# A new order of the vector and scalar engines' work, and a later inverse transfer, in the softmax attention of a two-block kernel

## The reference

```
first block:  stick-breaking attention (8 heads), and "MLA" attention (8 heads):
    z = q k^T * 96**-0.5 ; p = softmax(where(allowed, z, -inf)) ; o = p v
    y_mla = (o * silu(gate_mla)) @ w_o_mla
second block: "fox" attention (16 heads of 64):
    s = q k^T + c_q - c_k ; masked to k_pos <= q_pos ; p = softmax(s) ; o = p v ; m = o @ w_out
then MLPs, a short convolution, gates and norms
```

## Time and profile before

| | |
|---|---|
| time, median of 3 runs | 1698.45 us (1698.14 to 1699.87) |
| profiled execution | 1698.45 us, its span 1696.5 us |
| busy share of the span | PE 99%, PEld 85%, DVE 76%, ACT 56%, POOL 10% |
| granted TensorE clock | 0.998, 9 tenths or more in all 40 slices of the page |
| exponentials (L2197) | 96, the first at 300.2 us, the last at 659.6 us |
| spread inverses (L2219) | 24 transfers, 311.0 to 664.2 us |

### The profile page before, as it was taken

One profiled execution on the slowest core, in us unless ns is written; L12 is line 12 of the kernel. 1 busy time (PEld: TensorE's weight loads), 2 busy tenths in 40 slices (PEclk: granted clock), 3 DMA queues, 4 the chain that ended last, 5 costly groups with the idle time before them and its releaser, 6 DMA issues.

```text
span 1696.5 us, 25098 instructions
## 1 busy us (share of the span) xinstructions
PE 1673.9 (99%) x9279; PEld 1440.2 (85%) x9279; DVE 1287.2 (76%) x2054; ACT 951.4 (56%) x1717; POOL 169.8 (10%) x147
## 2 busy tenths in 40 slices
PE   9999999999999999999999999999999999999998
PEld 7888877888788887789999997778887989999977
DVE  6378877876568888688888986685556969898966
ACT  4267875665436666476646365642125766564555
POOL 2011212000300000310000002320003000000041
PEclk9999999999999999999999999999999999999999
DMA  8222124324243333344232343323232432332621
GB/s 269 86 75 75 40 69 107 85 66 149 75 113 88 87 89 94 94 176 128 75 105 95 125 174 112 112 75 100 99 99 107 156 100 100 100 108 92 242 69 50
DMA packets 158163, 180.72 MB, mean 107 GB/s; under 512 B 22121, under 2 KB 130182, under 8 KB 156262
## 3 DMA queue, kind: packets, MB, share of 16 engines
q1 hardware_dynamic: 150790, 159.22, 30.0%
q10 hardware_dynamic: 7264, 20.05, 3.4%
HBM read 161.96 MB, written 12.63 MB: 103 GB/s over the span
## 4 chain that ended last, share of the span: by engine, by line
PE 81%; DVE 10%; ACT 3%; DMA 3%; issue 2%; POOL 1%; DVEq 0%; ACTq 0%; POOLq 0%; SPq 0%
PE bank L1171 24%; PE bank L1172 23%; PE bank L1173 23%; DVE split_weights L2701 2%; DMA raw_weights<-in_w_mlp_down 2%; PE bank L1520 2%; PE bank L1544 1%; PE bank L1439 1%; POOL ssum L3663 1%; DVE act_b L2701 1%; PE bank L1557 1%; DMA inverse_rows<-row_sums 1%; PE bank L1428 1%; DVE act_a L2703 1%; PE bank L1556 0%
## 5 line engine op out<-in xcount | busy, mean ns | idle before, releaser
L1171 PE MATMUL bank<-act_a,split_weights 128*128 128x512 f32 (+1 forms) x1360 | 525.5, 386 | 4.6 <-ACT work L2183 1.4
L1173 PE MATMUL bank<-act_a,split_weights 128*128 128x512 f32 (+1 forms) x1360 | 518.5, 381 | 0.0
L1172 PE MATMUL bank<-act_a,split_weights 128*128 128x512 f32 (+1 forms) x1360 | 518.2, 381 | 0.0
L1171 PEld LDWEIGHTS bank<-act_a,split_weights 128*128 128x128 f32 x1360 | 256.0, 188 | 57.2 <-issue 6.0
L1173 PEld LDWEIGHTS bank<-act_a,split_weights 128*128 128x128 f32 x1360 | 255.6, 188 | 50.3
L1172 PEld LDWEIGHTS bank<-act_a,split_weights 128*128 128x128 f32 x1360 | 256.0, 188 | 44.9 <-issue 0.2
L1171 PE MATMUL bank<-act_b,split_weights 128*128 128x256 f32 (+1 forms) x648 | 207.4, 320 | 2.0 <-DVE split_weights L3395 1.5
L1173 PE MATMUL bank<-act_b,split_weights 128*128 128x256 f32 (+1 forms) x648 | 206.4, 318 | 0.0
L1172 PE MATMUL bank<-act_b,split_weights 128*128 128x256 f32 (+1 forms) x648 | 206.3, 318 | 0.0
L2643 DVE TENSOR_TENSOR split_weights<-raw_weights,split_weights 128x2048 fp32r<-128x2048 f32 x55 | 127.8, 2324 | 76.2 <-ACT split_weights L1882 63.4
L1882 ACT ACTIVATE split_weights<-raw_weights 128x2048 fp32r<-128x2048 f32 x51 | 97.3, 1908 | 119.6 <-PE bank L1173 119.6
(11 more groups left out here) (357 smaller groups left out, 3223.5 us busy)
## 6 DMA issues: line engine op xcount, KB each, us to landing
raw_weights<-in_w_mlp_up SPq DMA_DIRECT2D x32, 1024.0 KB, 5.4
raw_weights<-in_w_mlp_down SPq DMA_DIRECT2D x32, 1024.0 KB, 5.2
raw_weights<-in_w_in SPq DMA_DIRECT2D x18, 1024.0 KB, 5.1
raw_weights<-in_w_conv_in SPq DMA_DIRECT2D x12, 1024.0 KB, 5.1
raw_weights<-in_w_attn_in SPq DMA_DIRECT2D x16, 512.0 KB, 5.1
raw_weights<-in_w_ple_gate SPq DMA_DIRECT2D x8, 1024.0 KB, 5.0
raw_weights<-in_w_out SPq DMA_DIRECT2D x4, 1024.0 KB, 5.9
raw_weights<-in_w_attn_in SPq DMA_DIRECT2D x4, 1024.0 KB, 5.2
```

What stands on the lines that cost most here:

```text
L1171: nc.tensor.matmul(dst, w[0], a[0], start=first, stop=False)
L1172: nc.tensor.matmul(dst, w[0], a[1], start=False, stop=False)
L1173: mm = nc.tensor.matmul(dst, w[1], a[0], start=False, stop=last)
```

## The change

Three things change, and PE's strings are not among them.

A new step f on ACT issues the second head's b transfer of the pair before (it does nothing in pair 0). It stands after p1 (after e2 in fox, after e1 in fox's last pair), and b1 goes from the end of all pairs but MLA's last and fox's last, where it stays.

DVE's k moves from before p2 or m5 to behind m6, and other steps change places around it. In MLA c3 now stands ahead of m7, in fox y1 ahead of p4. Fox's last pair gets new strings on both engines, and output tile 2 (o2) moves into it from the pair before.

The two semaphores of the d transfers become one, which counts all of them.

```
-        inverse_out = [sem(f"inverse_out_{hh}") for hh in range(2)]
+        inverse_out = sem("inverse_out")
...
-        DVE_MLA = "m0 m1 m2 m3 p0 p1 k0 p2 m4 p3 n0 m5 c0 c1 c2 y1 m6 p4 m7 c3 p5 s2 n1 p6 g0 p7 y2 x0 x1 s3 g1"
+        DVE_MLA = "m0 m1 m2 m3 p0 p1 p2 m4 p3 n0 m5 c0 c1 c2 y1 m6 p4 k0 c3 m7 p5 s2 p6 n1 g0 p7 y2 x0 x1 s3 g1"
...
-        DVE_FOX = "m0 m1 c0 m2 c1 p0 m3 s2 p1 m4 k0 m5 p2 p3 n0 y0 m6 c2 m7 c3 p4 p5 y1 n1 g0 p6 p7 x0 x1 s3 g1"
+        DVE_FOX = "m0 m1 c0 m2 c1 p0 m3 s2 p1 m4 m5 p2 p3 n0 y0 m6 k0 c2 m7 c3 y1 p4 p5 g0 n1 p6 p7 x0 x1 s3 g1"
...
-                    act.wait_ge(inverse_out[hh], 16 * (h // 2 + 1))
+                    act.wait_ge(inverse_out, 16 * (h + 1))
...
+                        elif what == "f":
+                            if pair:
+                                inverse_to_half(pair - 1, s)
```

More of the change, by code:

```diff
@@ L460, in hybrid_block_kernel @@
         PE_MLA = "z0 g0 z1 g1 z2 t0 z3 t1 z4 g2 t2 z5 t3 z6 g3 v0 t4 z7 g4 t5 t6 g5 t7 g6 g7 v1"
-        ACT_MLA = "e0 e1 y1 p0 e2 p1 w0 e3 p2 p3 s2 w1 d0 e4 e5 p4 y2 e6 p5 e7 b0 p6 r0 p7 d1 s3 r1 b1"
-        DVE_MLA = "m0 m1 m2 m3 p0 p1 k0 p2 m4 p3 n0 m5 c0 c1 c2 y1 m6 p4 m7 c3 p5 s2 n1 p6 g0 p7 y2 x0 x1 s3 g1"
+        ACT_MLA = "e0 e1 y1 p0 e2 p1 f1 w0 e3 p2 p3 s2 w1 d0 e4 e5 p4 y2 e6 b0 p5 e7 p6 r0 p7 s3 d1 r1"
+        DVE_MLA = "m0 m1 m2 m3 p0 p1 p2 m4 p3 n0 m5 c0 c1 c2 y1 m6 p4 k0 c3 m7 p5 s2 p6 n1 g0 p7 y2 x0 x1 s3 g1"
@@ L463, in hybrid_block_kernel @@
         PE_FOX = "z0 g0 z1 g1 z2 t0 t1 z3 g2 z4 t2 g3 z5 t3 g4 z6 t4 t5 z7 v0 g5 t6 t7 g6 g7 v1"
-        ACT_FOX = "w0 y0 e0 e1 w1 p0 e2 s2 p1 e3 p2 p3 e4 e5 y1 d0 e6 s3 p4 p5 e7 r0 d1 p6 b0 p7 r1 b1"
-        DVE_FOX = "m0 m1 c0 m2 c1 p0 m3 s2 p1 m4 k0 m5 p2 p3 n0 y0 m6 c2 m7 c3 p4 p5 y1 n1 g0 p6 p7 x0 x1 s3 g1"
+        ACT_FOX = "w0 y0 e0 e1 w1 p0 e2 f1 s2 p1 e3 p2 p3 e4 e5 d0 y1 e6 s3 p4 p5 b0 e7 r0 p6 p7 d1 r1"
+        DVE_FOX = "m0 m1 c0 m2 c1 p0 m3 s2 p1 m4 m5 p2 p3 n0 y0 m6 k0 c2 m7 c3 y1 p4 p5 g0 n1 p6 p7 x0 x1 s3 g1"
@@ L468, in hybrid_block_kernel @@
         PE_NEAR = "z0 z1 z2 g0 g1 t0 t1 z3 g2 z4 t2 z5 g3 t3 z6 g4 t4 t5 v0 g5 z7 g6 g7 t6 t7 a0 v1"
-        ACT_NEAR = "y0 e0 e1 p0 p1 e2 w0 w1 e3 p2 p3 e4 e5 e6 d0 o0 o1 p4 p5 y1 r0 e7 o2 b0 p6 p7 d1 s2 r1 b1"
-        DVE_NEAR = "m0 m1 m2 k0 m3 p0 y0 c0 c1 p1 p2 m4 m5 p3 n0 m6 c2 c3 o0 o1 p4 y1 m7 p5 g0 x0 x1 n1 p6 p7 s2 o2"
+        ACT_NEAR = "y0 e0 e1 p0 p1 f1 e2 w0 w1 e3 p2 p3 e4 d0 e5 e6 o0 o1 p4 p5 b0 y1 r0 e7 p6 p7 s2 d1 r1"
+        DVE_NEAR = "m0 m1 m2 m3 p0 y0 c0 c1 p1 p2 m4 m5 p3 n0 m6 k0 c2 c3 o0 o1 p4 y1 m7 p5 g0 x0 x1 n1 p6 p7 s2"
@@ L473, in hybrid_block_kernel @@
         PE_LAST = "z0 z1 z2 g1 t0 z3 t1 g2 t2 t3 z4 z5 z6 g3 t4 z7 g4 v0 t5 g5 t6 t7 g6 v1"
[L474 to L478, removed]
+        ACT_LAST = "e0 s1 p0 e1 f1 y0 e2 o2 e3 p1 o3 w0 p2 y1 o4 p3 e4 o5 d0 w1 e5 o6 e6 e7 b0 p4 p5 d1 r0 p6 p7 b1 r1"
@@ L479, in hybrid_block_kernel @@
+        DVE_LAST = "m0 m1 m2 h1 p0 m3 s1 o2 y0 p1 o3 c0 p2 m4 o4 k0 y1 p3 n0 o5 m5 c1 m6 m7 c2 n1 c3 p4 p5 o6 g0 p6 p7 g1"
+        ACT_MLA_LAST = "e0 e1 y1 p0 e2 p1 f1 w0 e3 p2 p3 w1 d0 e4 e5 p4 o0 e6 b0 p5 o1 e7 p6 r0 d1 p7 o2 b1 r1"
+        DVE_MLA_LAST = "m0 m1 m2 m3 p0 p1 p2 m4 p3 n0 m5 c0 c1 c2 y1 m6 p4 k0 c3 m7 p5 o0 n1 p6 g0 o1 p7 x0 x1 o2 g1"
         EARLY_OUT = {"mla": 3, "fox": 7}
@@ L2211, in inverse_to_row @@
                     nc.scalar.dma_start(inverse_rows[hh, :].rearrange("(p j) -> p j", p=P), pair_sums(i, hh))\
-                        .then_inc(inverse_out[hh], 16)
+                        .then_inc(inverse_out, 16)
                 def inverse_to_half(i, hh):
                     h = heads_before(kind, 2 * i + hh)
-                    act.wait_ge(inverse_out[hh], 16 * (h // 2 + 1))
+                    act.wait_ge(inverse_out, 16 * (h + 1))
                     if i:
```

## The result

| | before | changed |
|---|---|---|
| time, median of 5 runs each | 1698.45 us (1698.14 to 1699.87) | 1707.88 us (1706.91 to 1708.19) |
| profiled execution, its span | 1698.45 us, 1696.5 | 1708.22 us, 1706.3 |

The ratio is 1.0052 with a 95% interval of 1.0038 to 1.0067, which is 6.5 to 11.4 us. The changed kernel is slower, as forecast, but by 9.4 us between the medians and not by 5.0, and 1707.88 lies above the forecast range. The time before is the median of 5 runs, not of 3 as the table ahead of the prediction has it.

The account below looks back on a forecast made before the run. PE, busy 99% of the span, was taken to bound the kernel. Terms 3.45 + 2.0 - 0.95 + 0.5 = +5.0 us on 1698.45 gave 1703.4 us (chance 0.50), range 1696.5 to 1707.

Parts of the forecast that it names:

- MLA, +3.45 forecast: MLA pairs 1 to 3: k and c3 ahead of m7 make t7 late by 1.15 us each, 3 x 1.15 = +3.45.
- it adds nothing: MLA, ACT: b0 waits for k and holds p5 until about 351.6, still earlier than m7, so no cost.
- Fox pairs 1 to 5, +2.0 forecast: Fox, DVE: k behind m6 and y1 ahead of p4 make t6 wait for p4; 0.4 us a pair, +2.0.
- the 0.2 at t7: Fox pairs: about 0.2 us that t7 waited for e7, claimed to be over once t6 starts later.
- b1 becomes f1, -0.95: Fox pair 3: f1 stands late enough that the d transfer is back, -0.95 us; all other pairs 0.
- Pair 6, 0 forecast: Pair before fox's last: o2 leaves, k moves behind m6, DVE had idle time; 0, within 0.3 us.
- Pair 7, +0.5 forecast: Fox's last pair: a new wait at g2 against a better ordered end; first share at 668.9 less 0.2, +0.5 us.
- The wait at g2: Fox's last pair: PE stands still some 2.6 us at g2 for o2's low part, ready at 654.2.
- the 13.3 us from g2 to v1: Fox's last pair: PE's time from g2 to v1, 13.3 us or a little less, putting v1 at about 667.5.
- is better ordered: End of fox's last pair: y1 early and weight quarters ahead of p4 remove v1's 1.44 us wait and 0.26 at 668.18.
- the last pair is worse: Rival, chance 0.16: g2 waits 2.6 us in fox's last pair and later steps do not close up; +7.1, 1705.5 us.
- Behind pair 7, 0 forecast: After fox's last pair: no cost given; weight quarters ahead of p4 were to remove a wait of 0.26 us.

Follow-up runs that it names:

- f1_behind: Changed kernel with f1 behind p2 instead of behind p1 on ACT in MLA; 1707.87 us, ratio 1.0058.
- m7_first: Changed kernel with DVE's row maximum m7 ahead of k and c3 again in MLA; 1709.64 us, ratio 1.0058.
- b0_behind: As m7_first, but on ACT in MLA b0 stands behind p5 and e7 instead of ahead of them; 1707.04 us, ratio 1.0047.
- y1_behind: Changed kernel with DVE's y1 behind p5 instead of ahead of p4 in fox's pairs 0 to 5; 1705.17 us, ratio 1.0038.
- e5_first: Changed kernel with e5 ahead of d0 on ACT in fox's pair 6; 1706.98 us, ratio 1.0047.
- c3_late: Changed kernel with DVE's c3 behind p7 instead of ahead of p4 in fox's pair 7; 1706.72 us, ratio 1.0050.

## Why the prediction was wrong in size

**MLA, +3.45 forecast, +4.3 measured.** The mechanism held: m7 starts at 352.70 where the text had 351.7 for the old start of the pair, which is 0.84 later now, and t7 waits 1.17 and 1.18 us where 1.15 was forecast. Two things were missed. f1's issue takes 0.45 us of ACT, ahead of w0 and e3, which costs 0.5 us over the three pairs (f1_behind). And in pair 3 o1 stands in front of e7, which costs 0.2; no run takes it away. The prediction's sentence on b0, that "it adds nothing", was right for this order only: with m7 ahead of k it becomes the bound (m7_first, b0_behind).

**Fox pairs 1 to 5, +2.0 forecast, +2.4 measured.** t6 waits 0.69 where the text had 0.6, and the 0.2 at t7 goes, as it said. y1_behind shows y1's share: without it t6 waits 0.34 less.

**b1 becomes f1, -0.95.** Right: pair 3 is as long as its neighbours, and no pair gained otherwise.

**Pair 6, 0 forecast, +0.7 measured.** The text looked at o2 and k only. It did not look at d0, which the new string puts ahead of e5, where it waits for n0 (e5_first).

**Pair 7, +0.5 forecast, +2.8 measured.** This is the step that failed. The wait at g2 was forecast as 2.6, and t1 and g2 together start 2.84 later. v1's wait is gone, as forecast. The failed term is the 13.3 us from g2 to v1, which rest on the sentence that the end of the pair "is better ordered": they took 15.16. t6 waits 1.1 us, for p4 behind b0 and c3. And behind the wait at g2 the clock fell, 1.4 us, for which the sum had no term. Without the clock the pair would be +1.4, and the rival "the last pair is worse" (+2.6) names the right mechanism for it.

**Behind pair 7, 0 forecast, +1.75 measured.** The text said that the weight quarters ahead of p4 take a wait of 0.26 away. It did not follow their semaphore: it releases SP's loads, which then ran beside d1's and b1's transfers (c3_late). d1 took 2.8 us instead of 1.4, so b1 was issued later, and b1 took 6.0 instead of 4.8. The 1.75 is the size in this execution; kernels with the same order there waited 0.76 to 2.23 us. The Trainium skill's page "DMA: Bandwidth & Descriptors", section "Queues, rings and completion order", says that a transfer engine takes turns between the queues that have work for it, so a small transfer shares the engines with a large one beside it. The traces agree in direction: b1 took 6.0 us beside the loads and 2.8 where it was issued ahead of them (c3_late).

Of the excess of 4.4 us in the medians, pair 7 and what lies behind it hold 2.3 + 1.75, MLA and fox 1 to 6 another 2.0, and the start and the stretch behind MLA give 1.3 back. The last 0.4 is the difference between the spans and the medians.

## What to carry to other kernels

Where engines run in a written order, read for each moved step also what it releases and which queue it holds: a transfer that waits on an engine's queue holds that engine's next work, and a weight split that ends early starts a load that competes with small transfers. A new place for a step is free only in a gap of the timeline that lies behind the last thing that PE needs soon. And a wait of the matrix engine can cost more than its length: of the 15 waits of 1.9 us and more in the traces above, the clock fell behind 11, and at g2 that cost about 1.4 us more.

## What the runs showed of the hardware

**The clock.** Behind a wait of 0.6 and one of 2.2 us, with 0.4 us of matmuls between them, the granted clock fell to the lower level in six of nine profiled executions with the same program order at that place. The Trainium skill's page "TensorE: Matmul & The Clock Gate", "Part 1: The HAM clock gate", describes a gate with two states that follows how busy the array was. The traces agree: 0.43 us between matmuls of 512 columns at a granted clock of 0.50, 0.23 at 1.00, and full clock in both kernels in which matmuls without use filled the wait.

**Small transfers.** In pair 7 the 2 KB transfer d1 took 1.4 us before, 2.2 in c3_late and 2.8 in the changed kernel. d0 took 1.4 us before and 3.4 in the changed kernel, because y1, which now ends early, releases another load of 512 KB (L1044) that SP issues at 666.64, 0.7 us ahead of d0. In the kernel before that load came at 664.09, behind both d's. All twelve kernels with the new end of the last pair have d0 at 3.3 to 3.6 us. b1's transfer of 128 KB took 2.8 us in c3_late, 4.8 before and 3.5 to 6.7 in the others of these twelve. An issue on ACT's queue takes 0.33 us (d) or 0.45 (b and f), and what stands behind it on ACT starts after it: 642.18 + 0.33 and e5 at 642.55.
